# Three feed-forwards cut into parts of 8, 8 and 6 tiles, with the second down job of each part in a spare bank

## The reference, cut to what matters

```python
# first block (called ffn0 in the kernel)
gt, up = jnp.split(jnp.einsum("bsd,df->bsf", h, w_ffn_up[l]), 2, axis=-1)
x = x + g2 * jnp.einsum("bsf,fd->bsd", jax.nn.silu(gt) * up, w_ffn_down[l])
# second block, twice (ffn1, ffn2), with a causal convolution of 3 taps over the gates
a, b = jnp.split(h @ w_up, 2, axis=-1)
a = sum(conv_w[j] * a_pad[:, j:j + S] for j in range(CONV_WIDTH_2)) + conv_b
return (jax.nn.silu(a) * b) @ w_down
```

## Time and profile before

| | |
|---|---|
| time, median of 3 runs | 2094.66 us (2092.9 to 2097.76) |
| profiled execution, its own time | 2093.53 us |
| its span in the profile | 2091.7 us |
| mean granted TensorE clock | 0.998 of full speed |
| PE busy | 2059.9 us, 98% of the span |
| PE weight loads busy | 1735.8 us, 83% |
| DVE, ACT, POOL busy | 989.1, 885.9, 840.6 us (47%, 42%, 40%) |
| DMA | 220.17 MB, mean 105 GB/s |

### The profile page before, as it was taken

One profiled execution on the slowest core, in us unless ns is written; L12 is line 12 of the kernel. 1 busy time (PEld: TensorE's weight loads), 2 busy tenths in 40 slices (PEclk: granted clock), 3 DMA queues, 4 the chain that ended last, 5 costly groups with the idle time before them and its releaser, 6 DMA issues.

```text
span 2091.7 us, 28578 instructions
## 1 busy us (share of the span) xinstructions
PE 2059.9 (98%) x10618; PEld 1735.8 (83%) x10618; DVE 989.1 (47%) x1909; ACT 885.9 (42%) x1307; POOL 840.6 (40%) x273
## 2 busy tenths in 40 slices
PE   9999999999999999999999999999999999999998
PEld 6888977888888888876877888888887588888887
DVE  4889788574311111376985344034323934431432
ACT  3355545463443222534366453233423954432332
POOL 3443422444244444433713443444443044444443
PEclk9999999999999999999999999999999999999999
DMA  9654322325232432432202433333422034324322
GB/s 371 243 185 125 102 62 66 101 85 178 81 100 81 114 107 78 113 93 65 79 24 64 113 100 93 107 105 94 143 86 73 2 96 121 100 80 121 100 70 91
DMA packets 304008, 220.17 MB, mean 105 GB/s; under 512 B 13520, under 2 KB 288080, under 8 KB 301616
## 3 DMA queue, kind: packets, MB, share of 16 engines
q1 hardware_dynamic: 293216, 195.67, 31.1%
q10 hardware_dynamic: 10704, 23.33, 3.7%
HBM read 213.48 MB, written 2.10 MB: 103 GB/s over the span
## 4 chain that ended last, share of the span: by engine, by line
PE 85%; DVE 7%; issue 3%; ACT 2%; POOL 2%; DMA 0%; ACTq 0%; DVEq 0%; SPq 0%; POOLq 0%
PE bank L912 72%; PE bank L1159 2%; PE bank L1375 2%; PE bank L1353 2%; DVE arena L2811 1%; PE bank L1307 1%; DVE small L2809 1%; PE bank L1362 1%; PE bank L1458 1%; PE bank L1207 1%; POOL w_split_out L2851 1%; DVE bank L2277 1%; POOL w_split L2851 1%; PE bank L1218 1%; PE bank L1540 1%
## 5 line engine op out<-in xcount | busy, mean ns | idle before, releaser
L912 PE MATMUL bank<-h_hi,w_split 128*128 128x512 f32 x3696 | 1119.4, 382 | 1.8 <-DVE arena L2679 1.1
L2851 POOL TENSOR_TENSOR w_split<-wslots,w_split 128x2048 fp32r<-128x2048 f32 (+3 forms) x174 | 712.7, 4097 | 987.9 <-ACT w_split L1613 549.5
L912 PEld LDWEIGHTS bank<-h_hi,w_split 128*128 128x128 f32 x3696 | 698.7, 189 | 116.8 <-issue 15.7
L912 PE MATMUL bank<-h_lo,w_split 128*128 128x512 f32 x1848 | 701.8, 380 | 0.0
L912 PEld LDWEIGHTS bank<-h_lo,w_split 128*128 128x128 f32 x1848 | 349.7, 189 | 51.2 <-issue 3.4
L912 PE MATMUL bank<-hid_hi,w_split 128*128 128x512 f32 x1056 | 316.2, 380 | 2.2 <-DVEq L2562 2.2
L1634 ACT ACTIVATE w_split<-wslots 128x2048 fp32r<-128x2048 f32 (+2 forms) x80 | 141.4, 1767 | 368.0 <-PE bank L912 368.0
L1613 ACT ACTIVATE w_split<-wslots 128x2048 fp32r<-128x2048 f32 (+3 forms) x91 | 158.8, 1745 | 300.8 <-PE bank L912 278.9
L912 PEld LDWEIGHTS bank<-hid_hi,w_split 128*128 128x128 f32 x1056 | 199.6, 189 | 32.3 <-issue 3.6
L912 PE MATMUL bank<-hid_lo,w_split 128*128 128x512 f32 x528 | 200.1, 379 | 0.0
L2277 DVE SCALAR_TENSOR_TENSOR bank<-arena,cols,bank 128x512 f32<-128x512 f32 x240 | 161.3, 750 | 5.4 <-ACT bank L1727 4.9
(11 more groups left out here) (341 smaller groups left out, 2352.4 us busy)
## 6 DMA issues: line engine op xcount, KB each, us to landing
wslots<-in_f_w_up SPq DMA_DIRECT2D x88, 512.0 KB, 4.7
wslots<-in_w_in SPq DMA_DIRECT2D x24, 1024.0 KB, 5.3
wslots<-in_w_ffn_up SPq DMA_DIRECT2D x44, 512.0 KB, 4.5
arena<-in_w_ada ACTq DMA_DIRECT2D x8, 2048.0 KB, 9.1
wslots<-in_f_w_down SPq DMA_DIRECT2D x16, 768.0 KB, 4.8
wslots<-in_a_w_in SPq DMA_DIRECT2D x10, 1024.0 KB, 5.2
wslots<-in_f_w_down SPq DMA_DIRECT2D x16, 640.0 KB, 4.4
arena<-in_w_ada_first SPq DMA_DIRECT2D x8, 1024.0 KB, 19.3
```

The lines of the kernel that those rows point to most:

```text
L912: return nc.tensor.matmul(bank[:], w, woven(x), start=start, stop=stop)
L2851: last = nc.gpsimd.tensor_tensor(part[:, 1, cols_of], slot(p, 1, size)[:, 0, cols_of], part[:, 0, cols_of].bitcast(F32), ALU.subtract)
```

## The change

`HALVES = ((0, 12), (12, 10))` becomes `PARTS = ((0, 8), (8, 8), (16, 6))`. Each feed-forward now has three up stages and three down stages. The hidden buffers hold 8 tiles instead of 12.

All down stages go through `first_downs`, and its order is another: all tiles but the last of job 0, all but the last of job 1, the last of job 0, the last of job 1. Job 1 no longer waits for its parity's `bank_free`, since it is computed in bank 2p + 1, the second bank of job 0's parity p, which down jobs leave unused (`down_bank`).

In the up stages ACT and POOL split the weights of odd jobs in two halves, and ACT does its first step of the hidden tile (Silu in ffn0, the convolution's first tap in the others) between them. Loops of PE, ACT, DVE and POOL over the jobs of these stages are written out. `up_acc` shares its memory with `up_gate`.

The diff also brings code for a scheme with seven instead of eight block products (`seven_products`, `three_sums`, `early_sums`, `token_sums_made` and so on). It is taken only for feed-forwards named in `SEVEN`, and `SEVEN = ()`: none of it is issued. What it leaves in the program are renamed semaphores, other places of constants in memory, and 24 unused columns and 136 unused constants that are loaded with the rest.

```diff
-HALVES = ((0, 12), (12, FT - 12))
+PARTS = ((0, 8), (8, 8), (16, FT - 16))
+LAST = len(PARTS) - 1
+SEVEN = ()
...
+        def down_bank(name, j):
+            return banks[2 * one(name, 0)[0] + 1] if name[:3] == "ffn" and j == 1 else banks[2 * one(name, j)[0]]
...
                 def tiles(q, first, end):
                     for c in range(first, end):
-                        if q == p:
-                            pe.wait_ge(S[waits[0]], waits[1] + c + 1)
+                        pe.wait_ge(S[waits[0]], waits[1] + c + 1)
                         for wp, hp in ((0, 0), (0, 1), (1, 0)):
-                            last = product_of(banks[2 * q], w[q][wp][:, c, :], rhs(c, hp), c == 0 and wp + hp == 0, c == kc - 1 and wp == 1)
+                            last = product_of(banks[2 * p + (q != p)], w[q][wp][:, c, :], rhs(c, hp), c == 0 and wp + hp == 0, c == kc - 1 and wp == 1)
                     if end == kc:
                         last.then_inc(product_done[q], 1)
 
-                for j, (q, first, end) in enumerate(((p, 0, kc - 1), (other, 0, 3), (p, kc - 1, kc), (other, 3, kc))):
-                    if j < 2:
-                        start_split(name, j)
-                    tiles(q, first, end)
+                start_split(name, 0)
+                tiles(p, 0, kc - 1)
+                pe.wait_ge(lo_ready[other], SPLITS_BEFORE[FIRST[name] + 1] + 1)
+                tiles(other, 0, kc - 1)
+                tiles(p, kc - 1, kc)
+                tiles(other, kc - 1, kc)
...
             def ffn(k):
-                for half, (t0, n) in enumerate(HALVES):
-                    name = f"ffn{k}_up{half}"
-                    if half or k == 0:
-                        split_product(name, DT, 2 * P, h_parts, None if half else ("norm_ready", TILES_BEFORE["ffn0"]))
-                    else:
-                        late_product(name, f"ffn{k}")
-                    waits, tiles_of = ("hid_ready", 2 + FT * k + t0), lambda c, part: hid[part][:, c, :]
-                    if k and half:
-                        first_downs(f"ffn{k}_down{half}", n, tiles_of, waits)
-                    else:
-                        split_product(f"ffn{k}_down{half}", n, P, tiles_of, waits, tiles=1)
+                for part, (t0, n) in enumerate(PARTS):
+                    up_part(k, part)
+                    first_downs(f"ffn{k}_down{part}", n, lambda c, half: hid[half][:, c, :], ("hid_ready", 2 + FT * k + t0))
...
+                        if i + 1 < tiles // 2:
+                            act.wait_ge(weights_in[p], LOADED[ahead])
+                            act.wait_ge(product_done[p], use + 1)
+                            first, second = slice(0, SLOT // 2), slice(SLOT // 2, SLOT)
+                            raw = slot(p, 1, SLOT)[:, 0, :]
+                            nc.scalar.activation(w_split[p][:, 0, first], raw[:, first], ACT.Copy).then_inc(S["softplus_then_sums_upper"], 1)
+                            conv_or_gate(2 * i + 1, p, use)
+                            nc.scalar.activation(w_split[p][:, 0, second], raw[:, second], ACT.Copy).then_inc(hi_ready[p], 1)
+                        else:
+                            split_job(ahead)
+                            conv_or_gate(2 * i + 1, p, use)
+                        gate_and_upper(2 * i + 1, p, following)
...
+                    if part < LAST:
+                        for j in range(DT):
+                            n = slot_after(FIRST[down] + j)
+                            if seven_at(k, part + 1, 0) and n == FIRST[f"ffn{k}_up{part + 1}"]:
+                                ...
+                            else:
+                                split_job(n)
```

More of the change, by code:

```diff
@@ L55 @@
 SPREADS = 5 + HEADS
-HALVES = ((0, 12), (12, FT - 12))
+PARTS = ((0, 8), (8, 8), (16, FT - 16))
+LAST = len(PARTS) - 1
+SEVEN = ()
 def ffn_stages(k):
-    return [(f"ffn{k}_{what}{half}", jobs) for half, (_, n) in enumerate(HALVES) for what, jobs in (("up", n), ("down", DT))]
+    return [(f"ffn{k}_{what}{part}", jobs) for part, (_, n) in enumerate(PARTS) for what, jobs in (("up", n), ("down", DT))]
 STAGES = [
@@ new lines, in sum_counts @@
+def sum_counts():
+    n, at = 4, {}
+    for k in SEVEN:
+        at[k] = n
+        n += 4
+        for part, (_, tiles) in enumerate(PARTS):
+            for i in range(-1, tiles // 2):
+                if seven_at(k, part, i + 1) and (i >= 0 or part):
+                    at[k, part, i + 1] = n
+                    n += 4
+                if seven_at(k, part, i) and k == 0:
+                    n += 1
+                    at[k, part, i, "late"] = n
+    return at
+UPPER, SUMS = upper_counts(), sum_counts()
@@ new lines, in late_sums @@
+            def late_sums(k, part, i):
+                q, use = one(f"ffn{k}_up{part}", 2 * i)
+                first, sums = up_gate[:, 1 - q, :], up_gate[:, q, :]
+                gates, ups = banks[2 * q], banks[2 * q + 1]
+                dve.wait_ge(product_done[q], use + 1)
+                steps.settle()
+                steps.did(nc.vector.tensor_tensor(gates[:, LOW], gates[:, LOW], first[:, LOW], ALU.add))
+                steps.did(nc.vector.tensor_tensor(gates[:, HIGH], gates[:, HIGH], sums[:, HIGH], ALU.add))
+                steps.did(nc.vector.tensor_tensor(ups[:, LOW], ups[:, LOW], sums[:, LOW], ALU.add))
+                last = nc.vector.tensor_tensor(ups[:, HIGH], banks[7][:, HIGH], sums[:, LOW], ALU.add)
+                if k:
+                    steps.did(last)
+                else:
+                    last.then_inc(S["angle_then_sum_ready"], 1)
+                    dve.wait_ge(S["angle_then_sum_ready"], SUMS[k, part, i, "late"])
+                steps.settle()
@@ L2752, in ffn, with turn @@
             def ffn(k):
-                for half, (t0, tiles) in enumerate(HALVES):
+                if k in SEVEN:
+                    token_sums_made(k)
+                for part, (t0, tiles) in enumerate(PARTS):
                     w3, _ = conv3_of(k, t0, tiles)
-                    for i, u, p, use in pairs(dve, f"ffn{k}_up{half}"):
-                        if u == 0:
-                            steps.loop(i, 2)
-                        t = 2 * i + u
+                    def turn(t, between):
+                        p, use = one(f"ffn{k}_up{part}", t)
                         n = FT * k + t0 + t
@@ L2772, in ffn @@
                         dve.wait_ge(S["ups_scaled"], n - FT + 1)
-                        hidden(n, t, tiles, p, use)
-                    steps.end_loop(tiles // 2)
-                    if half == 0:
-                        residual(f"ffn{k}_down0", 1)
+                        hidden(n, t, p, between)
+                    up_part(k, part, turn)
+                    if part < LAST:
+                        down_sums(k, part)
                 if k == 1:
-                    late_dve(dve, steps, "b_mix", "ffn1_down1")
+                    late_dve(dve, steps, "b_mix", f"ffn1_down{LAST}")
                 else:
-                    residual("ffn2_down1", 1, None, "last")
+                    residual(f"ffn2_down{LAST}", 1, None, "last")
             def turned_tables(first, done):
```

390 lines of the change are left out of this document (331 added, 59 removed).

## The result

| | before | after |
|---|---|---|
| median | 2095.97 us (4 runs, 2092.9 to 2097.76) | 2157.18 us (4 runs, 2150.18 to 2159.92) |
| ratio | | 1.0289, 95% interval 1.0259 to 1.0318 |
| profiled execution | 2093.53 us, span 2091.7 | 2159.92 us, span 2158.1 |
| granted clock | 0.998 | 0.989 (the other runs 0.990, 0.994, 0.991) |

The change made the kernel 61 us slower. The forecast was 2153. The page of the changed kernel shows the span, the busy times and, in its fifth part, the matmuls of the down jobs (columns as before; the last numbers are the idle time ahead and who ended it).

What follows compares the result with a forecast made beforehand. TensorE, in flight 98% of the span, was taken as the bound. Waits of 46.2 us and 12 us of clock on the profiled 2093.53 gave 2151.7, so 2153 us as median; 8 in 10 for 2135 to 2166.

Steps and rivals of the forecast that it cites:

- step 1: First two down jobs: PE waits for the refill of job 0's split buffer, 3.45 us in six 8-tile stages, 20.8 us.
- step 2: Down to up: PE waits 1.95 us for a 2048-column refill at six places, 11.7 us; the weight load stays hidden.
- step 3: Last down stage of ffn0: 6-tile jobs don't hide the 4.45 us bank chain, then the refill for `a_keys`: +8.9 us.
- Step 4: Last down stages: ffn1 loses 3.35 us at its first wait and 1.05 ahead of `b_mem`; ffn2 loses 2.7.
- signs of being wrong: Missing waits behind job 0, a wait for a load (DMA), or up stages at another pace than 10.36 us a job.
- Step 5: Last hidden tile of ffn1 and ffn2: earlier waits shrink, 0.25 us left in each, a gain of 2.3 us.
- Step 6: 24 more residual sums, written-out loops, halved splits, 160 more constant columns: taken at nothing, a us at most if any shows.
- Step 7: Clock: seven of the ten waits of 2.5 to 3.8 us followed by half speed, none of six short ones: 12 us.
- the forecast's own case: Waits of 46.2 us and 12 us of clock: 2153 us, own range 2146 to 2158, chance 0.5.
- rival B: Clock falls after every long wait and some of six short ones, 10 to 16 drops: 2158 to 2168 us, chance 0.17.
- rival A: Waits as forecast, but the clock stays at full speed: 2141 us (2136 to 2145), chance 0.2.
- Rival C: The refill doesn't bind, only the two 1.1 us waits go: 2092 us; chance 0.04, shared with an unseen reason for coming out even.

Runs made afterwards that it cites:

- e2_order: Changed kernel with more of job 1 behind job 0's last tile (plain job order in ffn0, half of job 1 in ffn1 and ffn2): 2128.46 us, ratio 1.0158.
- e5_two_parts: Changed kernel with two parts of 12 and 10 tiles instead of three, its order of the first two down jobs kept: 2133.81 us, ratio 1.0182.
- e3_parts: Kernel before, with its own order of the down jobs, in three parts of 8, 8 and 6 tiles: 2142.57 us, ratio 1.0227.
- e6_split_last: Changed kernel with ACT's split of b_q's first weights moved behind job 6's upper part and squares in ffn1's last down stage: 2151.02 us, ratio 1.0263.
- e7_fitted: Changed kernel in two parts (12, 10), with 1 or 2 tiles of job 1 ahead of job 0's last: 2090.94 us against 2094.0, ratio 0.9980.
- e4_spare: Kernel before with the spare bank alone, in the last halves of ffn1 and ffn2, and tiles reordered there: 2091.8 us against 2094.74, ratio 0.9985.
- e1b_fill: Changed kernel with 3, 2 or 1 matmuls of unread result put into PE's waits, shorter than the waits: 2145.62 us, ratio 1.0242.

## Why the prediction was right, and where it was off

Steps 1, 2 and 3 held: 19.4, 10.1 and 8.5 us against 20.8, 11.7 and 8.9. They are a little high, since I added 0.15 us to each wait for a slow restart on top of the 0.05 from POOL to PE; the starts in the trace show 3.23 and 1.68 where 3.31 and 1.81 were worked out without it. Taking the refill in the kernel before from the one place where it was just late was what made the sizes come out. e2_order and e5_two_parts show that it is the refill: its wait grows by 0.35 to 0.41 us a tile and shrinks by what is left of job 1. e3_parts shows that the parts have a price of their own.

Step 4 failed at its end: `b_mem` waited 5.5 us, not 1.05. The prediction checked that the loads of the up stages stay hidden (step 2). For `b_q` it counted ACT's split in chain 6, but not the wait for the raw weights, which held ACT for 5.03 us; e6_split_last shows that this is what PE waited for. A wait for a load is one of the signs of being wrong that the prediction names; here it came on ACT. The sizes of ffn2's stage and of ffn1's first wait were 0.3 us high.

Step 5: the two waits went, 2.5 us, and the leftover of 0.25 us was not seen in ffn1's and ffn2's last stages. The last hidden tile was ready there 6.2 us after the start of the down stage, not 6.7. At equal width it comes 0.3 us earlier in the changed kernel too (6.58 us in e5_two_parts, 6.88 before, for 10 tiles), which the prediction left out.

That the sum of the waits came out (46.5 us against 46.2) is luck: 4.45 us too little for `b_mem` and 4.15 too much in the other rows cancel.

Step 6 held, as far as e7_fitted tests it: it has the written-out loops, halved splits and constants, though not the 24 residual sums of the third parts, and is as fast as e4_spare.

Step 7 was the right mechanism at too small a size: seven drops behind ten long waits were taken, eight behind eleven were seen; but three of them lasted twice 3.4 us, and two more fell in the attention, which has the same waits of 1.9 and 0.5 us before. The cost was 20.5 us instead of 12; over the four runs the cost varies with the clock (2150.18 us at 0.994, 2159.92 at 0.989). e1b_fill shows that it is the standing still that costs it. Since the waits cancel, the clock is the forecast's distance from the profiled execution (8.5 of 8.2 us). The median, 2157.18 us, is in the range of the forecast's own case (2146 to 2158), but only just: of the four runs two lie in it (2150.18 and 2155.35 us) and two in rival B's (2159.02, and the profiled one of 2159.92 us with ten stretches; B had 10 to 16 drops, 2158 to 2168). None came near rival A. Of B's two parts neither came true as written, since three of the long waits were followed by no drop and none of the short ones by one.

Rival C, a refill that doesn't bind, is excluded by the 3.06 us waits put down to POOL. Left open is why some of the waits of one length are followed by half speed and others not; no run here separates it.

## What to carry to other kernels

Before moving a tile or cutting a stage, work out what each job hides: with one split buffer for each parity, job n + 1 must be as long as the refill behind job n, and an order that ends both jobs together leaves only the last tile for it. On this kernel a bank that comes free earlier is worth no more than the wait it removes, here 2.5 us. Price a wait of TensorE with the half-speed time behind it (in the profiled execution here another 0.44 us for each us of wait, 20.5 for 46.5), and look at what stands behind a load in an in-order queue before a stage is made shorter.

## What was not expected of the hardware

A half-speed stretch can be 6.8 us instead of 3.4 (three of the ten in the changed kernel, two of them behind waits of 3.06 and 3.07 us like those that have 3.4 us or none). A matmul of 512 columns on plain float32 operands, not in the split format, showed as two records 0.43 us apart, 0.86 us, four times the 0.2158 us of the kernel's own. A 1 MB load took 9.3 us instead of 5.1 when a 2 MB load was issued 3.3 us ahead of it, and 7.2 us when it was 5.9.
